# A 31-tap depthwise convolution shared out anew among ScalarE, GpSimd and VectorE inside a two-network kernel

## What is computed

```python
def conv_module(z, dw_w, dw_b, ln_g, ln_b):
    a, gate = jnp.split(z, 2, axis=-1)
    y = a * jax.nn.sigmoid(gate)
    y = lax.conv_general_dilated(y, dw_w[:, None, :], window_strides=(1,),
        padding=[(CONV_PAD, CONV_PAD)], dimension_numbers=("NWC", "WIO", "NWC"),
        feature_group_count=CONV_DIM) + dw_b          # 31 taps, each channel by itself
    y = layer_norm(y.reshape(b, s, CONV_GROUPS, CONV_GROUP_DIM), ...)
    return jax.nn.silu(y)

def spatial_gating(z, ln_g, ln_b, w_s, b_s):
    z = jax.nn.gelu(z, approximate=False)
    u, v = jnp.split(z, 2, axis=-1)
    v = layer_norm(v, ln_g, ln_b)
    mixed = jnp.einsum("hpq,bnqhc->bnphc", w_s, v) + b_s.T[...]
    return u * mixed.reshape(b, s, SGU_DIM)

z = h @ ab_w_in
x = x + jnp.concatenate([y_conv, y_sgu], axis=-1) @ ab_w_out
```

## Time and profile before

| | us |
|---|---|
| median of three runs | 3438.58 |
| the profiled execution, as timed | 3441.41 |
| its span, first to last instruction | 3439.6 |
| TensorE busy over the span | 3218.2 |
| VectorE busy | 2137.7 |
| ScalarE busy | 1387.3 |
| GpSimd busy | 474.6 |
| product with `ab_w_in`, first to last matmul | 1441.67 to 1647.06 |
| first matmul of the product with `ab_w_out` | 1700.22 |

### The profile page before, as it was taken

The page is one execution under the profiler, slowest core; times in us unless marked ns, Lnnn a source line. Parts: engine busy times, 40 slices in busy tenths (PEclk is TensorE's granted clock), DMA queues, the critical chain, the costliest instruction groups (busy, mean ns, idle before and its releaser), DMA issues.

```text
span 3439.6 us, 54280 instructions
## 1 busy us (share of the span) xinstructions
PE 3218.2 (94%) x22453; PEld 2782.7 (81%) x22453; DVE 2137.7 (62%) x1863; ACT 1387.3 (40%) x1435; POOL 474.6 (14%) x350
## 2 busy tenths in 40 slices
PE   5787789799999999798799999999999999999998
PEld 3445578688888888698698888888889888888888
DVE  7668755655555565669766565665645665665554
ACT  4446634443333333333344434433334443443333
POOL 2979710000000000069100000000000000000000
PEclk7889999899999999899899999999999999999999
DMA  9998875345555555344155555555534555555552
GB/s 292 301 312 245 247 261 181 132 168 187 183 193 185 186 191 184 101 163 163 56 196 185 186 192 180 186 195 183 184 128 147 196 184 193 177 179 201 190 183 86
DMA packets 351038, 643.33 MB, mean 187 GB/s; under 512 B 21600, under 2 KB 50360, under 8 KB 350520
## 3 DMA queue, kind: packets, MB, share of 16 engines
q1 hardware_dynamic: 309952, 561.42, 49.6%
q10 hardware_dynamic: 40951, 79.98, 6.9%
HBM read 637.29 MB, written 4.06 MB: 186 GB/s over the span
## 4 chain that ended last, share of the span: by engine, by line
PE 82%; DVE 6%; DMA 4%; issue 3%; ACT 2%; POOL 2%; SPq 1%; DVEq 0%; ACTq 0%; POOLq 0%
PE acc L466 43%; PE acc L467 25%; PE acc L463 4%; PE acc L464 4%; DMA raw<-in_w_mod_dram 2%; DVE w_lo L890 1%; DVE z L1134 1%; PE acc L1356 1%; DMA tw<-r_scratch 1%; DMA r_scratch<-rw 1%; POOL cpow L2009 1%; PE acc L1448 1%; ACT u L1610 1%; POOL ptmp L2009 1%; PE acc L1431 0%
## 5 line engine op out<-in xcount | busy, mean ns | idle before, releaser
L890 DVE TENSOR_TENSOR w_lo<-raw,w_hi 128x2048 fp32r<-128x2048 f32 x484 | 1107.9, 2298 | 985.0 <-ACT w_hi L696 985.0
L696 ACT ACTIVATE w_hi<-raw 128x2048 fp32r<-128x2048 f32 x484 | 924.0, 1914 | 1253.2 <-PE acc L467 1253.0
L466 PE MATMUL acc<-hid,w_hi 128*128 128x512 f32 x3840 | 1357.4, 399 | 0.0
L467 PE MATMUL acc<-xin,w_lo 128*128 128x256 f32 x3968 | 1115.6, 281 | 0.0
L467 PE MATMUL acc<-hid,w_lo 128*128 128x256 f32 x3840 | 1078.3, 281 | 0.0
L466 PE MATMUL acc<-xin,w_hi 128*128 128x512 f32 x2496 | 871.4, 393 | 8.8 <-DVE xin L915 8.8
L466 PEld LDWEIGHTS acc<-hid,w_hi 128*128 128x128 f32 x3840 | 721.5, 188 | 179.9
L467 PEld LDWEIGHTS acc<-xin,w_lo 128*128 128x128 f32 x3968 | 752.0, 190 | 0.0
L467 PEld LDWEIGHTS acc<-hid,w_lo 128*128 128x128 f32 x3840 | 725.3, 189 | 0.1
L466 PEld LDWEIGHTS acc<-xin,w_hi 128*128 128x128 f32 x2496 | 471.2, 189 | 113.6 <-issue 9.2
L463 PE MATMUL acc<-xin,w_hi 128*128 128x256 f32 x1472 | 417.4, 284 | 23.8 <-DVE w_lo L890 15.6
(11 more groups left out here) (275 smaller groups left out, 2184.5 us busy)
## 6 DMA issues: line engine op xcount, KB each, us to landing
raw<-in_ffn_w_gate_dram SPq DMA_DIRECT2D x88, 1024.0 KB, 5.2
raw<-in_ffn_w_up_dram SPq DMA_DIRECT2D x88, 1024.0 KB, 5.2
raw<-in_ffn_w_down_dram SPq DMA_DIRECT2D x88, 1024.0 KB, 5.0
raw<-in_w_mod_dram ACTq DMA_DIRECT2D x76, 1024.0 KB, 9.8
raw<-in_w_mlp_in_dram SPq DMA_DIRECT2D x64, 1024.0 KB, 5.2
raw<-in_w_mlp_out_dram SPq DMA_DIRECT2D x64, 1024.0 KB, 5.0
raw<-in_s_w_glu_dram SPq DMA_DIRECT2D x32, 1024.0 KB, 5.4
raw<-in_ab_w_in_dram SPq DMA_DIRECT2D x32, 1024.0 KB, 5.3
```

The source lines that it names most:

```text
L466: pe.matmul(bank, w_hi[:, slot, w], operand[:, kt, :], start=first, stop=False)
L467: ins = pe.matmul(bank[:, 0:TOK], w_lo[:, slot, w], operand[:, kt, 0:TOK], start=False, stop=last)
L696: act.activation(w_hi[:, slot, :], raw[:, slot, :, :].rearrange("p k n -> p (k n)"), ACT.Copy).then_inc(hi_ready, 1)
L890: dve.tensor_tensor(w_lo[:, slot, :], raw[:, slot, :, :].rearrange("p k n -> p (k n)"), w_hi[:, slot, :].bitcast(F32), SUB).then_inc(lo_re ...
```

## The change

Tiles 0 to 3 now belong to ScalarE and GpSimd, tiles 4 to 7 to VectorE.

- ScalarE multiplies four tiles by one tap in four Identity activations with a scale per partition (`tap`), the first tap with the bias straight into `z`, the others into a half of `tmp`. A tap from the fourth on waits until GpSimd has added the one two before it. The 31 taps are dealt out behind the 23 `w_hi` copies of loops 2 to 7 (loop 7's fourth excepted): one or two behind each.
- GpSimd adds a whole tap, 128 x 1024, in one TENSOR_TENSOR: 30 adds.
- VectorE no longer convolves in loops 2 and 3; `conv_in`'s second half is made in loop 3, and its 31 taps of four tiles are done in loops 3 to 6, eight, eight, eight and seven.
- In the mixer no taps are left. The convolution's sums and centring come directly behind those of `v`, its variance behind that of `v`, and its reciprocal root before the gating. The squares of `v` go to `v_sq` (in `xin`), since `tmp` holds taps.

```diff
-        CONV_POOL = 2
+        CONV_POOL = 4
@@ TensorE, mixer
                 ins.then_inc(v_mean, 1)
+                pe.wait_ge(conv_dve, (8 - CONV_POOL) * W_CONV)
+                pe.wait_ge(conv_pool, W_CONV - 1)
+                for k in range(8):
+                    ins = pe.matmul(ps[k // 2][:, ...], ones, z[:, k, :], start=True, stop=True)
+                ins.then_inc(conv_mean, 1)
                 pe.wait_ge(v_sqd, 1)
...
                 ins.then_inc(v_var, 1)
+                pe.wait_ge(conv_sqd, 1)
+                for k in range(8):
+                    ins = pe.matmul(ps[4][0:8, 0:TOK], one_column[k], conv_sq[:, k, :], start=(k == 0), stop=(k == 7))
+                ins.then_inc(conv_var, 1)
...
                 pe.wait_ge(v_ms, 1)
+                pe.wait_ge(conv_ms, 1)
...
             def spread_conv_rstd():
                 pe.wait_ge(conv_rs, 1)
+                pe.wait_ge(gated, 2)
@@ ScalarE
+            def tap(w):
+                for k in range(CONV_POOL):
+                    x, c = conv_in[:, k, w:w + TOK], par[:, ...]
+                    if w == 0:
...
+                        ins = act.activation(z[:, k, :], x, ACT.Identity, scale=c, bias=par[:, ...])
+                    else:
+                        if k == 0 and w > 2:
+                            act.wait_ge(conv_pool, w - 2)
+                        ins = act.activation(tmp[:, w % 2, k, :], x, ACT.Identity, scale=c)
+                ins.then_inc(conv_mul, 1)
...
+            for j in range(8):
+                for slot in range(SLOTS):
+                    if j == 7 and slot == 3:
+                        evacuate(j)
+                    split(G + 1 + j, slots=(slot,))
+                    upto = min(W_CONV, -(-W_CONV * (4 * (j - 2) + slot + 1) // 23)) if j >= 2 else 0
+                    while done < upto:
+                        tap(done)
+                        done += 1
+                if j in (1, 3, 4, 5, 6):
+                    evacuate(j)
@@ VectorE
             for j in range(8):
                 split(G + 1 + j)
...
-                if j == 2:
...
-                    convolve(first_half, 0, 16)
-                if j == 3:
-                    convolve(first_half, 16, W_CONV)
-                if j == 4:
-                    dve.wait_ge(folded, AB_IN[1] + 4)
+                if j == 3:
+                    dve.wait_ge(folded, AB_IN[1] + 4)
...
-                if j >= 4:
-                    convolve(second_half, 7 * (j - 4), min(7 * (j - 3), 24))
+                if 3 <= j < 7:
+                    convolve(second_half, 8 * (j - 3), min(8 * (j - 2), W_CONV))
@@ GpSimd
+            for w in range(1, W_CONV):
+                pool.wait_ge(conv_mul, w + 1)
+                if w > 1:
+                    pool.wait_ge(conv_pool, w - 1)
+                pool.tensor_tensor(z[:, 0:CONV_POOL, :], z[:, 0:CONV_POOL, :], tmp[:, w % 2], ALU.add).then_inc(conv_pool, 1)
```

More of the change, by code:

```diff
@@ L213, in two_layer_kernel @@
         y_sqs = [sq_h, sq_x]
+        v_sq = sq_x[:, 0:8, :]
         QZ = 8 * KB
@@ L523, in mixer @@
                 pe.wait_ge(v_sb, 1)
[L524 to L528, removed]
                 for h in range(8):
@@ L827, in GEMM_ACT, with evacuate @@
             G = AB_IN[0] // 4
[L828 to L831, removed]
+            def tap(w):
+                for k in range(CONV_POOL):
+                    x, c = conv_in[:, k, w:w + TOK], par[:, cols["dw_w"] + 8 * w + k:cols["dw_w"] + 8 * w + k + 1]
+                    if w == 0:
+                        if k == 0:
+                            act.wait_ge(conv_in_ready, 1)
+                            act.wait_ge(pad_zero, 1)
+                        ins = act.activation(z[:, k, :], x, ACT.Identity, scale=c, bias=par[:, cols["dw_b"] + k:cols["dw_b"] + k + 1])
+                    else:
[3 more added lines that the diff above has]
+                ins.then_inc(conv_mul, 1)
+            def evacuate(j):
                 place, func = {1: (8, ACT.Sigmoid), 3: (12, ACT.Sigmoid)}.get(j, (4 * j, ACT.Gelu))
@@ L835, in GEMM_ACT @@
                 act.activation(z[:, place:place + 4, :], sums[j % 2], func).then_inc(folded, 1)
+            done = 0
+            for j in range(8):
[9 more added lines that the diff above has]
+                    evacuate(j)
+            assert done == W_CONV
             act.wait_ge(ws_tr, 1)
@@ L1134, in convolve @@
                         dve.scalar_tensor_tensor(z[:, k, :], x, c, z[:, k, :], MUL, ADD).then_inc(conv_dve, 1)
-            first_half, second_half = range(CONV_POOL, 4), range(4, 8)
+            second_half = range(4, 8)
             for j in range(8):
@@ L1177, in GEMM_DVE @@
             ins.then_inc(v_out, 1)
-            convolve(second_half, 28, W_CONV)
-            dve.wait_ge(conv_mean, 1)
-            dve.scalar_tensor_tensor(zc.rearrange(flat), lower, -1.0 / P, zc.rearrange(flat), MUL, ADD).then_inc(conv_centred, 1)
+            dve.wait_ge(conv_root, 1)
+            dve.reciprocal(rs[0:8, 1, :], rs[0:8, 1, :]).then_inc(conv_rs, 1)
             for c in range(2):
@@ L1187, in GEMM_DVE @@
                 rest(xin, z[:, 16 + CH * c:16 + CH * (c + 1), :], chunk(2 + c), xin_ready)
[L1188 to L1191, removed]
             for c in range(2):
@@ L1216, in GEMM_POOL @@
             pool.tensor_tensor(conv_in[:, 0:4, PAD:PAD + TOK], z[:, 0:4, :], z[:, 8:12, :], ALU.mult).then_inc(conv_in_ready, 1)
[L1217 to L1230, removed]
-                        pool.tensor_tensor(z[:, k, :], z[:, k, :], conv_tmp[:, step % 2, :], ALU.add).then_inc(conv_pool, 1)
-                    step += 1
+            for w in range(1, W_CONV):
[3 more added lines that the diff above has]
+                pool.tensor_tensor(z[:, 0:CONV_POOL, :], z[:, 0:CONV_POOL, :], tmp[:, w % 2], ALU.add).then_inc(conv_pool, 1)
         block = ctx.enter_context(nc.Block())
```

20 lines of the change are left out of this document (11 added, 9 removed).

## The result

The changed kernel took 3444.4 us (median of 11 runs) where the kernel before, in turn with it on the same chip, took 3436.8 (11 runs): a ratio of 1.0026, 95% interval 1.0018 to 1.0034. By the ratio that is some 9 us (6 to 12; the medians are 7.6 apart), inside the range (3425 to 3452), and just over the 0.2% that I had called the limit of "no change". Its profiled execution, of 3441.5 us, happened to be as long as that of before (3441.4). Ratios are always against the kernel before on the same chip.

The account below looks back on a forecast made before the run. VectorE, late for TensorE in blocks 4 to 7, and the mixer's chain behind were taken as the bound; V 8.5 us later less 7.3 in the mixer gave +1.2 on 3438.6, rounded 3440 us, range 3425 to 3452.

Parts of the forecast that it names:

- The price of an add: Convolution: each 128x1024 GpSimd add takes 2.15 us from VectorE (0.6 to 2.46); 20 adds, 43.0 us.
- Rival 1: Convolution: GpSimd's long adds let VectorE in, costing 0.6 us each; 3409 us, or 3401 at no price; chance 0.08.
- rival 3: Convolution: each add costs VectorE its whole length and the restart, 2.6 us; 3449 or 3454 us; chance 0.20.
- VectorE's sum: From block 3's end to V, the scaling of v's sums: VectorE's work totals 131.7 us, V 8.5 us later.
- From there VectorE is never idle, because every `w_hi` it needs is made well ahead: From 1538.4 us, after block 3's Sigmoid, until V: VectorE works without a pause, 131.7 us.
- it keeps up: GpSimd needs 1.35 adds per 5.63 us slot and manages even with 2.2 us of waiting; costed at nothing.
- TensorE's waits: Before blocks 5, 6 and 7 TensorE waits for VectorE's low parts, some 13, 7 and 9 us.
- The mixer: From V to the next product's first unit: the new order takes 31.3 us against 38.6, -7.3 us.
- this question for v's sums: Mixer: whether TensorE comes warm to v's sums of squares, priced at 5.7 us; if warm, 2.1 us less.
- the clock -2 to +1: Mixer: the range's allowance for TensorE's clock, -2 to +1 us.
- No change: Whole kernel: a difference within 0.2%, 6.9 us, forecast at 3440 us; chance 0.57.
- The slower rival: Convolution: rival 3, each add costing VectorE 2.6 us, +9 us in all, 3449 us; chance 0.20.

Follow-up runs that it names:

- the gaps: Changed kernel, but VectorE's first instruction of each group of four taps waits for the group before, idling 0.25 us: ratio 1.0036.
- the three widths: Changed kernel with a 0.25 us VectorE pause ahead of each four taps, GpSimd adding 8, 512 or 1024 columns: ratios 0.9909, 0.9962, 1.0036.
- the two runs: 29 matmuls with unused results added in the mixer: on the changed kernel 1.0010, on the version where VectorE makes the 30 adds itself 0.9964.

## Why the prediction was right, and where it wasn't

**The price of an add** (2.15, bounds 0.6 and 2.46) held. In the changed kernel a tap caught by an add took 2.62 instead of 0.47 us, 2.15 more. On average over 20 adds it was 1.96 with the gaps. It came from one pair of 128x256, minus a constant overlap of 0.25 us; that this overlap stays the same at four times the width was taken on trust, and only the three widths showed it. Rival 1 (0.6 us) and rival 3 (2.6 us) both fall as mechanisms. The Trainium skill (SBUF — State Buffer, "SBUF: two separate sides") says that whoever starts first holds the shared pair for the whole instruction and the other fully blocks. The caught taps agree nearly: they lost 2.15 us of an add's 2.41, not all of it. What that sentence leaves open is who gets the pair when one engine issues without a pause, and that decided the waits here.

**VectorE's sum** (V 8.5 us later) was right at 9.2, but two of its parts were wrong and cancelled. "From there VectorE is never idle, because every `w_hi` it needs is made well ahead" failed: it was idle 5.84 and 5.85 us. For that, only 14 of the taps and low parts in this stretch were held for a full add (12 taps at 2.15 and two low parts at 2.2), and two more by 1.4. Held time 33.0 plus idle 11.7 is 44.7 us, where I had 43.0: the adds that GpSimd could not place among the taps fell into the idle time that they had caused. That the two come out within 1.7 us of each other was not forecast, and is luck. My "it keeps up" for GpSimd was the wrong step behind it. I had asked how much time GpSimd needs in a slot, not when it may start. The sign stood in a row that I had used: beside low parts a TENSOR_SCALAR on GpSimd had taken 5.08 us, where I allowed 2.2 us of waiting. The run with gaps bears the sum's own premise out: nothing idle but the gaps, and V moved by no more than these.

**TensorE's waits** were forecast as 13, 7 and 9 us before blocks 5, 6 and 7. Block 5 came on time, block 6 waited 22.5 us at once, block 7 not at all. Neither the places nor the sum (29 forecast) were right, by the same step: kept out, GpSimd let VectorE go first and was repaid later. With the gaps, where nothing of that is left but one add, they are 14.1, 8.4 and 6.4, 28.9 in all, as forecast. Less waiting of TensorE's did not bring V sooner, since V waits for VectorE.

**The mixer** was the term that was mis-sized. I gave the order -7.3 us. In the profiled execution of after it was -5.5 at the first unit: token mixing took 5.47 us, not 3.7, and v's sums 5.95 instead of 5.7. The old order has the convolution's sums directly ahead of the token mixing, on the same engine (5.23 us, then 3.58 for the mixing, in the run with the old order too). Taking them out of the middle let TensorE reach the mixing from an idle stretch. Of the ten other executions of the new order nine have 5.3 to 5.6 us there too. The tenth, with adds of 128x512, has the same 2.0 us of idleness ahead of the mixing, and 3.84 us for it. So the idle stretch goes with the lower clock, but doesn't settle where it falls. The row that I used for the mixing was not of the engine's state in the new order; I had asked this question for v's sums, and not for the mixing. A further 4.5 us were lost behind the first unit: the units then ran at half pace for a while (one matmul in 0.21 us where it is 0.12), with this row and those like it:

```profile
1708.89 0.51 PE acc L464
...
1709.62 0.21 PE acc L468
```

The granted clock says the same. A line of windows gives: stretch, length, busy time and count of TensorE's matmuls and weight loads, VectorE, ScalarE, GpSimd, granted clock, DMA share, GB/s. Here are the token mixing and the way from the first unit to the second block's end, before and then after:

```profile
1691.50:1695.30 3.80, 3.77 (x33) 3.55 (x32) 3.42 (x2) 1.24 (x1) 0.00 (x0) 1.00 0.00 0
1700.18:1749.48 49.30, 49.30 (x403) 48.36 (x403) 25.81 (x18) 23.62 (x24) 0.00 (x0) 1.00 0.39 129
```
```profile
1689.17:1694.72 5.55, 5.47 (x32) 5.28 (x32) 1.22 (x1) 1.08 (x2) 0.00 (x0) 0.69 0.00 0
1697.20:1751.00 53.80, 53.79 (x402) 52.52 (x403) 24.86 (x17) 23.18 (x23) 0.00 (x0) 0.90 0.36 119
```

TensorE has no wait on the second way in either. Over all thirteen traces its length follows the granted clock: 49.3 us at 1.00, 50.8 to 51.2 at 0.97 (three), 52.2 or 52.3 at 0.93 (three), 53.7 to 54.2 at 0.90 or 0.91 (six). The old order had 1.00 and 0.97, the new one 0.90 to 0.97. The windows of after, eight microseconds each, show the granted clock at 0.72 in this stretch, part of it at the lower level of 1.2 GHz, after two stretches in which TensorE was idle for 2.5 and 1.2 of 8 us:

```profile
1688.00:1696.00 8.00, 5.47 (x32) 5.28 (x32) 2.46 (x3) 2.25 (x2) 0.00 (x0) 0.79 0.00 0
1696.00:1704.00 8.00, 6.79 (x45) 6.82 (x46) 2.32 (x2) 2.34 (x2) 0.00 (x0) 0.79 0.00 0
1704.00:1712.00 8.00, 8.00 (x37) 6.72 (x36) 3.41 (x3) 4.13 (x8) 0.00 (x0) 0.72 0.01 2
```

I had allowed the clock -2 to +1; it took 1.9 at the mixing and 4.5 behind it (1.8 to 4.9 in the other executions of the new order). Where the lower clock falls differs from one execution to the next, also of one kernel (53.8 and 51.2 us for the two of the adds on VectorE). The 3.5 us or so by which the order gains at the second block's end (median V+85.1 of the ten, against 87.9 and 89.4) is a rough figure for that reason.

**The forecast as a whole.** With V at +9.2 and -1.0 for what is behind it, the sum is +8.2 instead of +1.2. "No change" was called at 0.57 and "slower" at 0.20; the interval, 0.18% to 0.34%, lies on the boundary and mostly beyond it. The slower rival gave a time near what was measured, by a price per add that the trace denies. The loss itself is VectorE's, 9.2 us, as forecast; what the forecast had too low, 7.0 us, is 0.7 of VectorE's and 6.3 of the mixer's and the two blocks' behind it, which gave back 1.0 and not 7.3. Why the whole is no gain was seen rightly: VectorE got rid of 60 taps and has to stand still for 20 adds of 2 us.

**Left open.** What decides whether a waiting add gets in ahead of VectorE's next instruction: no order in the starts holds through the traces, and none was tried. Whether a TensorE that is kept busy shortens the mixer: the two runs contradict each other within the scatter, and matmuls directly ahead of the token mixing or of the first unit, where it stands idle, were not tried.

## What to carry to other kernels

Before work is moved to an engine that shares a port with the one that is late, compare what the moved instruction will take away from that engine with what it costs there: 1.96 us against 1.13 for the add itself, and 1.6 for the whole multiply-and-add. Take the work apart, too: here the multiplying was worth giving to ScalarE, the adding was not worth giving to GpSimd. Ask of a helper not only how much time it needs but when it gets in, and who waits for it: behind 28 instructions without a gap an add of 2.4 us ended after 17.5, and the third engine's queue stood with it. And a step that is taken out from ahead of a matmul group was also what kept TensorE busy; price the group behind it by a row from after an idle stretch.

## What the runs showed that I had not expected

- GpSimd can be kept out for as long as VectorE issues without a pause: 17.5 and 13.7 us for single adds of 1024 columns, 11.9 to 13.5 us for four of 8 columns. A pause of 0.25 us once in four taps ended it beside the taps; beside four low parts it stayed.
- An add costs VectorE in proportion to its width (0.97 and 1.96 us for 512 and 1024 columns), and nothing measurable for 8. A tap caught by it loses the add's length less 0.25 us, at 256, 512 and 1024 columns.
- The distance between matmuls in the same product was 0.117 us in some executions and 0.119 in others, also of one and the same kernel (adds on VectorE: blocks 22.8 us apart in one execution, 22.5 in the other). That is 2 us over the stage. I have no cause for it.
